# Six orders of work on VectorE and ACT in a four-layer network kernel

## The reference

```
for l in range(2):                                     # first block
    x = x + 0.5 * swiglu(rmsnorm(x), w_in, w_out)      # feed-forward, inner width 2816
    x = x + hybrid_mixer(rmsnorm(x), ...)              # gated delta rule + stick-breaking attention
    x = x + 0.5 * swiglu(rmsnorm(x), w_in, w_out)
for l in range(2):                                     # second block
    x = x + 0.5 * swiglu_2(rms_norm(x), w_gate, w_up, w_down)
    x = x + hybrid_mixer_2(rms_norm(x), ...)           # MLA with rope, MoBA, dilated attention
    x = x + 0.5 * swiglu_2(rms_norm(x), ...)
return rms_norm(x, final_norm)
```

## Time and profile before

| | us |
|---|---|
| median of three runs (2608.71 to 2610.06) | 2609.12 |
| the profiled execution by itself | 2609.09 |
| its span in the profile | 2607.2 |
| PE busy | 2590.5 (99%) |
| PEld busy | 2211.3 (85%) |
| DVE busy | 2031.3 (78%) |
| ACT busy | 1545.2 (59%) |
| POOL busy | 116.4 (4%) |
| mean use of the 16 DMA engines by queue 1 | 54.9% |

### The profile page before, as it was taken

The page is one execution under the profiler, slowest core; times in us unless marked ns, Lnnn a source line. Parts: engine busy times, 40 slices in busy tenths (PEclk is TensorE's granted clock), DMA queues, the critical chain, the costliest instruction groups (busy, mean ns, idle before and its releaser), DMA issues.

```text
span 2607.2 us, 34896 instructions
## 1 busy us (share of the span) xinstructions
PE 2590.5 (99%) x14184; PEld 2211.3 (85%) x14184; DVE 2031.3 (78%) x2080; ACT 1545.2 (59%) x1703; POOL 116.4 (4%) x146
## 2 busy tenths in 40 slices
PE   9999999999999999999999999999999999999998
PEld 7889998888888899888888889978888888978887
DVE  8887854698799686557998995676997996677987
ACT  6556674465565567644656555555656555655654
POOL 0000170000000003400000000000000000000000
PEclk9999999999999999999999999999999999999999
DMA  7646545466465554545756465544755646544663
GB/s 235 234 151 202 164 144 182 139 225 228 150 231 173 171 163 158 184 133 179 237 167 231 161 204 183 161 144 155 242 194 183 212 162 189 160 146 145 215 230 105
DMA packets 353820, 473.99 MB, mean 182 GB/s; under 512 B 28726, under 2 KB 278910, under 8 KB 353406
## 3 DMA queue, kind: packets, MB, share of 16 engines
q1 hardware_dynamic: 349246, 469.86, 54.9%
q10 hardware_dynamic: 4416, 1.90, 0.3%
HBM read 466.09 MB, written 5.64 MB: 181 GB/s over the span
## 4 chain that ended last, share of the span: by engine, by line
PE 88%; DVE 4%; ACT 2%; POOLq 2%; issue 1%; DVEq 1%; DMA 1%; SPq 0%; POOL 0%; ACTq 0%
PE bank L420 27%; PE bank L422 27%; PE bank L421 27%; PE bank L1012 1%; DVE w_lo L407 1%; POOLq L2504 1%; ACT w_hi L401 1%; POOLq L2501 1%; DVE conv_acc L2264 1%; PE bank L1882 1%; PE bank L563 1%; DMA raw<-in_ffn_w_in 0%; DVEq L2268 0%; PE bank L2759 0%; PE bank L1806 0%
## 5 line engine op out<-in xcount | busy, mean ns | idle before, releaser
L420 PE MATMUL bank<-w_hi,xn_hi 128*128 128x512 f32 (+2 forms) x1856 | 704.9, 380 | 2.3 <-DVE xn_lo L535 1.4
L422 PE MATMUL bank<-w_hi,xn_lo 128*128 128x512 f32 (+2 forms) x1856 | 691.8, 373 | 0.0
L421 PE MATMUL bank<-w_lo,xn_hi 128*128 128x512 f32 (+2 forms) x1856 | 691.0, 372 | 0.0
L407 DVE TENSOR_TENSOR w_lo<-raw,w_hi 128x2048 fp32r<-128x2048 f32 (+2 forms) x190 | 412.9, 2175 | 220.7 <-ACT w_hi L401 220.2
L1135 ACT ACTIVATE w_hi<-raw 128x2048 fp32r<-128x2048 f32 x192 | 367.2, 1913 | 137.3 <-DMA raw<-in_ffn_w_out 39.5
L401 ACT ACTIVATE w_hi<-raw 128x2048 fp32r<-128x2048 f32 (+2 forms) x198 | 357.8, 1809 | 147.9 <-PE bank L422 146.7
L1243 DVE TENSOR_TENSOR w_lo<-raw,w_hi 128x2048 fp32r<-128x2048 f32 x192 | 438.0, 2281 | 1.0 <-ACT w_hi L1135 0.8
L420 PEld LDWEIGHTS bank<-w_hi,xn_hi 128*128 128x128 f32 x1856 | 349.7, 188 | 66.6 <-issue 5.4
L422 PEld LDWEIGHTS bank<-w_hi,xn_lo 128*128 128x128 f32 x1856 | 349.5, 188 | 61.6
L421 PEld LDWEIGHTS bank<-w_lo,xn_hi 128*128 128x128 f32 x1856 | 350.0, 189 | 56.3
L420 PE MATMUL bank<-w_hi,hid_hi 128*128 128x512 f32 x704 | 278.1, 395 | 0.0
(11 more groups left out here) (401 smaller groups left out, 3919.8 us busy)
## 6 DMA issues: line engine op xcount, KB each, us to landing
raw<-in_w_in SPq DMA_DIRECT2D x122, 1024.0 KB, 5.2
raw<-in_ffn_w_in SPq DMA_DIRECT2D x126, 512.0 KB, 5.2
raw<-in_ffn_w_out SPq DMA_DIRECT2D x44, 1024.0 KB, 5.3
raw<-in_ffn_w_down SPq DMA_DIRECT2D x44, 1024.0 KB, 5.2
raw<-in_ffn_w_gate SPq DMA_DIRECT2D x64, 512.0 KB, 4.5
raw<-in_ffn_w_up SPq DMA_DIRECT2D x64, 512.0 KB, 5.5
block<-in_ffn_w_in SPq DMA_DIRECT2D x48, 512.0 KB, 7.3
block<-in_ffn_w_gate SPq DMA_DIRECT2D x24, 512.0 KB, 6.8
```

The source lines that it names most:

```text
L407: dve.tensor_tensor(in_order(kind, slot, w_lo), as_loaded(kind, slot), in_order(kind, slot, w_hi).bitcast(F32), ALU.subtract).then_inc(s_l ...
L420: pe.matmul(out, a_hi, b_hi, start=start, stop=False, skip_group_check=check)
L421: pe.matmul(out, a_hi, b_lo, start=False, stop=False, skip_group_check=check)
L422: return pe.matmul(out, a_lo, b_hi, start=False, stop=stop, skip_group_check=check)
```

## The change

No instruction's shape changes but for one at the end; the order does. (1) `to_mixer_dve`: the mean square of tokens 128 to 255 goes in front of the second half of `split_lo_half` of item 1, four times. (2) `first_ones` in `ffn_dve`, eight times: the low half of block b11 goes behind both multiplications of unit 1. (3) `mixer1_dve`: at item 10 `split_lo` goes in front of the convolution. (4) `logs_dve` goes from the head of items 14 to 17 to items 13 to 16, behind the convolution and ahead of the sb sums and of `split_lo`; for the third and fourth it waits for `s_la`, since they reuse `De`. (5) `mixer2_dve`: the k rope goes one item ahead and its copies get a function of their own; `mixer2_act`: the copies of pair 3 go one item ahead, in front of a `split_hi`. (6) The end: the gain of chunk 2 goes behind the update of chunk 3, and chunk 3 gets gain and scale in one instruction.

```diff
@@ to_mixer_dve
             update(dve, q, 3, BY_ROWS)
+            mean_square_dve(dve, q, 1)
             split_lo_half(dve, p, 1, 1, s_lo)
-            mean_square_dve(dve, q, 1)
             scaled_gain_dve(dve, q, 1)
@@ ffn_dve, first_ones
                 sum_t1(2)
-                lo("b11", 2)
                 hide_from_bank(1, 0)
                 mixed_lo(2)
                 hide_from_bank(1, 1)
+                lo("b11", 2)
                 lo("dn", 1)
                 lo_hidden(1)
@@ mixer1_act, mixer1_dve
+        GATES_ACT = K0 + 7
-                if j == K0 + 7:
+                if j == GATES_ACT:
                     delta_gates_act(act, l)
...
-                if 0 <= j - PRODUCT0 < 4:
-                    logs_dve(dve, l, j - PRODUCT0)
...
+                if j == GATES_ACT:
+                    split_lo(dve, pm, j + 2)
                 if kind in "kqv":
                     conv_dve(dve, l, j)
+                if 0 <= j - SPREAD0 < 4:
+                    logs_dve(dve, l, j - SPREAD0)
                 if kind in ("sbq", "sbk"):
...
-                if 1 <= j <= LATE:
+                if 1 <= j <= LATE and j != GATES_ACT:
                     split_lo(dve, pm, j + 2)
@@ logs_dve
             dve.wait_ge(s_gb, l * 4 + (p + 1))
+            if p >= 2:
+                dve.wait_ge(s_la, l * 4 + (p - 1))
@@ mixer2_act
                 for p in pair_at(j - 2):
                     for e in range(2):
-                        copy_act(act, l, 2 * p + e)
+                        if p != 3:
+                            copy_act(act, l, 2 * p + e)
...
+                if 3 in pair_at(j - 1):
+                    for e in range(2):
+                        copy_act(act, l, 6 + e)
                 if j + 3 < N2:
                     split_hi(act, pm, j + 3)
@@ mixer2_dve
+                if j == UKV:
+                    rope_dve(dve, l, 0)
                 if j == UKV + 1:
-                    for i in range(2):
-                        rope_dve(dve, l, i)
+                    key_copies_dve(dve, l)
+                    rope_dve(dve, l, 1)
@@ rope_dve
             ins = dve.tensor_tensor(t, t, turned[rot, 0:m, :], ALU.add)
+            if i:
+                ins.then_inc(s_rope, 1)
             dve.drain()
-            if i == 0:
-                dve.wait_ge(s_upr, l * 8 + 6)
-                ins = dve.tensor_copy(km[64:96, :, :], kr[64:96, :].unsqueeze(1).to_broadcast([32, 6, T]))
-            ins.then_inc(s_rope, 1)
+        def key_copies_dve(dve, l):
+            dve.wait_ge(s_upr, l * 8 + 6)
+            dve.tensor_copy(km[64:96, :, :], kr[64:96, :].unsqueeze(1).to_broadcast([32, 6, T])).then_inc(s_rope, 1)
@@ the end of the vector list
-            def scaled_dve(t):
+            def last_rstd(t):
                 dve.wait_ge(s_root, roots(last_norm) + (t + 1))
                 dve.reciprocal(rstd[:, t:t + 1], root[:, t:t + 1]).then_inc(s_rstd, 1)
-                dve.drain()
-                dve.tensor_scalar(xg[:, 2 * t + 1, :], xg[:, 2 * t + 1, :], rstd[:, t:t + 1], None,
-                                  ALU.mult).then_inc(s_y, 1)
...
-            updated(2)
-            scaled_dve(0)
+            update(dve, last_norm, 2, BY_ROWS)
+            last_rstd(0)
             update(dve, last_norm, 3, BY_ROWS)
             mean_square_dve(dve, last_norm, 1)
-            gain_dve(dve, last_norm, 3, BY_ROWS)
-            scaled_dve(1)
+            dve.tensor_scalar(xg[:, 1, :], xg[:, 1, :], rstd[:, 0:1], None, ALU.mult).then_inc(s_y, 1)
+            gain_dve(dve, last_norm, 2, BY_ROWS)
+            last_rstd(1)
+            dve.drain()
+            dve.scalar_tensor_tensor(out=xg[:, 3, :], in0=x[:, 1, half(1)], scalar=rstd[:, 1:2], in1=gain[:, half(1)],
+                                     op0=ALU.mult, op1=ALU.mult).then_inc(s_y, 1)
```

## The result

The changed kernel takes 2612.55 us (median of 22 runs, 2611.77 to 2614.11), the kernel before 2608.68 (22 runs, 2607.99 to 2610.06). The ratio is 1.0015 with a 95% interval of [1.0009, 1.0021]: slower by 3.9 us, within the 0.2% that the prediction called no change, but the interval excludes an equal time. The forecast was 3.1 us slower.

A forecast was written before the change was run, and what follows sets the result against it. TensorE was taken to bound the kernel, with VectorE the local bound in the feed-forward stages. Terms: 7.05 us won, 10.2 lost, 3.1 slower than the 2609.12 median, forecast 2612.2 us, range 2603.5 to 2615.5.

The forecast's parts named there:

- TensorE bounds, VectorE locally: TensorE busy 2590.5 of 2607.2 us; VectorE busy 28.29 of 28.30 us through each feed-forward stage's first two-unit step.
- The wait of 1.5 us in seven stages, 0.6 in the first: In first_ones, VectorE idles this long before unit 1's second multiplication, waiting for ACT's second Silu.
- Slack 0.17, so 1.33 a stage: At sum u3, TensorE's next product has 0.17 us slack, so VectorE's 1.5 us lag costs 1.33.
- The first stage: Near 1 us won at unit 1's transposes is given back some 17 us later, and 0.6 lost on top.
- The mixers' gains: Low half before convolution 1.5 us, logarithms 1.75, rope 1.1, pair 3 copies 1.25, mean square 0.85 won.
- The rope term: Second-block mixer: k rope one item earlier removes TensorE's stall at the first q product, 0.56 x 2 = 1.1 us.
- the mean square: Ahead of the half split: 0.38 x 2 before second-block mixers, 0.05 twice before first-block ones; 0.85 us won.
- The end: ACT's last scaling goes from 2603.58 to 2602.96 and the store with it: 0.6 us won.
- The sum: Whole kernel: 7.05 us won, 10.2 lost, 3.1 us slower, forecast 2612.2.
- Rival (A): The wait for the Silu is harmless; the other terms and the first stage's 1 us show: 2601 us, chance 0.16.
- (B): Block edit costs as said, and the logarithms hurt in the sb columns at four places: 2616 us, chance 0.10.
- (C): Block edit's price per stage at its lower bound: 7 lost, 7 won, 2609 us; chance 0.74 together with likeliest case.

The follow-up runs named there:

- the short T3: Changed kernel with the sum T3 of the first two-unit step cut to 256 of 2048 columns in all eight stages: 2600.09 us, ratio 0.9968.
- both kernels that isolate the block edit: The kernel before with the b11 reordering alone: 2619.37 us, ratio 1.0042; the changed kernel with that reordering undone: 2601.76 us, ratio 0.9974.
- the kernel with the gap filled: Changed kernel with the low halves of mixed blocks 1 and 3 moved into VectorE's gap before the second multiplication: 2605.07 us, ratio 0.9986.

## Why the prediction was right, step by step

- **TensorE bounds, VectorE locally.** Right. The gap is harmless where the stretch behind it has room (the short T3), and expensive where it hasn't.
- **The wait of 1.5 us in seven stages, 0.6 in the first.** Right: 1.47 to 1.52, and 0.60. The strict order that the prediction read from the earlier trace rows holds here too: VectorE stood 1.47 us before a low half that it had computed in just this time before the change.
- **Slack 0.17, so 1.33 a stage.** The lag and the start of the product behind u3 came as computed (1.51 and 1.33). The step that was mis-sized is the subtraction: a stop also costs TensorE 0.08 at the product that follows, so 1.41. The prediction had met the effect (it put 0.08 on each stalled spread of the decays) and left it out where it counted losses. Over all stages the term was 10.2 and measured 10.7 alone and 10.8 within the change.
- **The first stage.** Right in kind and size: 0.98 won, given back, and 0.6 to 0.8 on top.
- **The mixers' gains.** Right: 6.45 forecast; 6.7 read from the offsets. The rope term lacked the same 0.08 a stall (0.56 forecast, 0.64 measured, at each first q product), and the mean square won 0.23 in front of the first block's mixers where 0.1 was forecast. The other edits together won 6.9 with the end, forecast 7.05.
- **The end.** Wrong as a term. ACT's scaling did come 0.57 earlier, but I took "and the store with it" for the whole, and the two stores that now begin together take longer to land: 0.16 in place of 0.6. It is too small to be told by the time.
- **The sum.** 3.9 against 3.1. The block edit was put 0.6 too low, the mixers' gains 0.3 too low and the end 0.4 too high, so the last two nearly cancel, by luck, and the restart's 0.6 is most of the difference.
- **Rival (A)** fell by the block edit alone (10.7 slower, not faster), **(B)** by the logarithms alone (no new wait in the sb columns), **(C)**, 7 us, by both kernels that isolate the block edit. The letters are those of the prediction.

What isn't settled: why TensorE's second product is late after a stop, what makes the two last stores slower, the 0.8 us wait for mla_q in the kernel with the logarithms alone, and why stages 2 and 4 lose 0.3 more than the others in the kernel with the gap filled.

## What to carry to other kernels

Before an instruction is put ahead of a long one on an in-order engine, ask when its input comes: the long one may be the very work that fills the wait, and the idle time is then paid at the end of the next stretch in which that engine has none to spare, however far off. A list of waits is no price list: the eight waits of 7.5 us cost 10.8, since small stops are hidden in the modelled ends and the product behind a stop comes late too, while a stall won where another engine sets the pace is worth nothing. Match the bounding engine's instructions one by one between two traces of equal order, and the offsets give each edit its own price, also those that no timing can tell from zero.

## What the runs showed of the hardware

- After a stop TensorE's second product follows 0.31 to 0.34 after the first, in place of 0.23, also where no idle time is shown (1459.94 to 1460.25). That is 0.08 to 0.11 a stop for products of 128x512 at the full granted clock.
- Two stores of 256 KB that start together took up to 2.9 us to land; started 0.23 apart, up to 2.5. A last result that is ready 0.57 earlier ended the program 0.16 earlier.
- One low half of 128x512 more, with a wait for its own end behind it, has a pitch of 0.76 us on VectorE (1439.67 to 1440.43) where its like without one has 0.60.
